# Prompt attention of a two-layer encoder step: the four query tiles of a head in the order 3, 0, 2, 1

## What is computed

```python
def mla_attend(q_nope, q_pe, q_pos, k_nope, k_pe, v, k_pos):
    s = jnp.einsum('bqhd,bkhd->bhqk', q_nope, k_nope) + jnp.einsum('bqhr,bkr->bhqk', q_pe, k_pe)
    s = s.astype(jnp.float32) * MLA_SCALE
    mask = (k_pos[None, :] // CHUNK) <= (q_pos[:, None] // CHUNK)
    s = jnp.where(mask[None, None], s, -jnp.inf)
    p = jax.nn.softmax(s, axis=-1).astype(v.dtype)
    return jnp.einsum('bhqk,bkhv->bqhv', p, v)
```

## Time and profile before

| | us |
|---|---|
| median of three runs | 2980.27 |
| lowest, highest | 2978.68, 2980.59 |
| profiled execution, its own time | 2978.17 |
| profiled execution, span | 2976.2 |

### The profile page before, as it was taken

How to read it: one execution, slowest core, us unless ns; L and a number is a source line. 1 busy time by engine, 2 the same in 40 slices (tenths; PEclk the granted TensorE clock), 3 DMA queues, 4 the chain that set the end, 5 groups by cost and what they waited for, 6 DMA issues and landing times.

```text
span 2976.2 us, 49155 instructions
## 1 busy us (share of the span) xinstructions
PE 2798.5 (94%) x18292; PEld 2660.1 (89%) x18292; DVE 1293.6 (43%) x2187; ACT 939.3 (32%) x1412; POOL 896.1 (30%) x362
## 2 busy tenths in 40 slices
PE   6899999989879989999989999998997998999997
PEld 4799999989867889999989999998986788999996
DVE  7742342462574353232364334245257535323234
ACT  6541221233344332111243222133334533211112
POOL 0233233343110233333343323334321113333333
PEclk8999999989989989999989999998998998999998
DMA  9533333322141112222224233332213201222223
GB/s 337 193 116 100 127 113 104 108 83 81 47 147 44 43 57 78 66 83 71 71 85 143 98 114 127 100 113 85 76 50 116 87 29 57 71 76 80 78 64 106
DMA packets 81891, 284.71 MB, mean 96 GB/s; under 512 B 9963, under 2 KB 12939, under 8 KB 81099
## 3 DMA queue, kind: packets, MB, share of 16 engines
q1 hardware_dynamic: 71307, 259.35, 26.6%
q10 hardware_dynamic: 10432, 23.27, 2.6%
HBM read 276.12 MB, written 6.46 MB: 95 GB/s over the span
## 4 chain that ended last, share of the span: by engine, by line
PE 88%; DVE 5%; issue 4%; ACT 2%; DMA 1%; ACTq 0%; SPq 0%; DVEq 0%
PE bank L887 24%; PE bank L889 24%; PE bank L888 24%; PE bank L896 5%; PE bank L1321 1%; PE bank L1282 1%; PE bank L908 1%; DVE n_lo L1434 1%; PE bank L1294 1%; DVE r_t L1751 1%; PE bank L1311 1%; DVE q_h L1755 1%; PE bank L1038 1%; PE bank L1040 1%; PE bank L1039 1%
## 5 line engine op out<-in xcount | busy, mean ns | idle before, releaser
L442 POOL TENSOR_TENSOR w_lo<-raw,w_hi 128x1024 fp32r<-128x1024 f32 x340 | 856.1, 2530 | 2064.3 <-ACT w_hi L483 2064.3
L887 PE MATMUL bank<-n_hi,w_hi 128*128 128x320 f32 x3264 | 1020.5, 313 | 56.9 <-DVE n_lo L1434 56.9
L888 PE MATMUL bank<-n_lo,w_hi 128*128 128x320 f32 x3264 | 1015.9, 311 | 0.0
L889 PE MATMUL bank<-n_hi,w_lo 128*128 128x320 f32 x3264 | 1015.6, 311 | 0.0
L887 PEld LDWEIGHTS bank<-n_hi,w_hi 128*128 128x128 f32 x3264 | 619.2, 190 | 66.8 <-DVE n_lo L1434 64.0
L888 PEld LDWEIGHTS bank<-n_lo,w_hi 128*128 128x128 f32 x3264 | 619.8, 190 | 1.9
L889 PEld LDWEIGHTS bank<-n_hi,w_lo 128*128 128x128 f32 x3264 | 619.4, 190 | 0.0
L483 ACT CAST w_hi<-raw 128x1024 fp32r<-128x1024 f32 x340 | 346.0, 1046 | 564.4 <-PE bank L889 511.4
L887 PE MATMUL bank<-h_hi,w_hi 128*128 128x320 f32 x1408 | 435.7, 309 | 0.0
L889 PE MATMUL bank<-h_hi,w_lo 128*128 128x320 f32 x1408 | 435.1, 309 | 0.0
L888 PE MATMUL bank<-h_lo,w_hi 128*128 128x320 f32 x1408 | 435.1, 309 | 0.0
(11 more groups left out here) (238 smaller groups left out, 2775.5 us busy)
## 6 DMA issues: line engine op xcount, KB each, us to landing
raw<-in_wmain SPq DMA_DIRECT2D x340, 512.0 KB, 3.6
araw<-in_wada SPq DMA_DIRECT2D x144, 512.0 KB, 4.9
pk_t<-in_pastkT ACTq DMA_DIRECT2D x16, 256.0 KB, 3.9
pv<-in_pastv ACTq DMA_DIRECT2D x16, 256.0 KB, 4.2
x<-in_xT SPq DMA_DIRECT2D x1, 2560.0 KB, 14.9
y<-y_sb SPq DMA_DIRECT2D x1, 2560.0 KB, 7.5
s_s<-in_s ACTq DMA_DIRECT2D x4, 512.0 KB, 4.1
uk_t<-in_ukT ACTq DMA_DIRECT2D x2, 1024.0 KB, 6.2
```

The lines of the kernel that those rows point to most:

```text
L442: pool.tensor_tensor(w_lo[slot][:], raw[slot % 2][:].rearrange("p (c m) -> p c m", m=P), w_hi[slot][:].bitcast(F32), ALU.subtract).then_in ...
L887: pe.matmul(out, w_hi[w][:, c, :], r_hi, start=first, stop=False)
L888: pe.matmul(out, w_hi[w][:, c, :], r_lo, start=False, stop=False)
L889: return pe.matmul(out, w_lo[w][:, c, :], r_hi, start=False, stop=last)
```

## The change

A function gives the query tile of a prompt tile, in the order 3, 0, 2, 1 within each head. The widths of the scores, maximum, exponential, scaling, transposes, copy and values follow it, and so does the place of the queries and of the outputs. The condition under which PE waits for a bank of the previous pair of heads is written by the tile's number, since the first tile of a head is no longer query tile 0. Banks, buffers, semaphores and the rounds of the casts stay as they are.

```diff
+        def q_tile(it):
+
+            return (3, 0, 2, 1)[(it - NDEC) % 4]
...
-                            w = P * ((it - NDEC) % 4 + 1)
+                            w = P * (q_tile(it) + 1)
...
-                            qt = (jt - NDEC) % 4
+                            qt = q_tile(jt)
...
-                        h, qt = (it - NDEC) // 4, (it - NDEC) % 4
+                        h, qt = (it - NDEC) // 4, q_tile(it)
...
-                    src, n = (p_s[it % 4], 3) if it < NDEC else (p_p[it % 4], (it - NDEC) % 4 + 1)
+                    src, n = (p_s[it % 4], 3) if it < NDEC else (p_p[it % 4], q_tile(it) + 1)
...
-                    if h % 2 == 0 and qt == 0:
+                    if (it - NDEC) % 8 == 0:
...
-                            t = p_p[n][:, 0:P * ((jt - NDEC) % 4 + 1)]
+                            t = p_p[n][:, 0:P * (q_tile(jt) + 1)]
```

## The result

| | before | after |
|---|---|---|
| median of 20 runs | 2979.64 | 2983.82 |
| lowest, highest | 2976.9, 2984.7 | 2980.66, 2990.41 |
| profiled execution, its own time | 2978.17 | 2990.41 |
| first prompt scores to output projection, layer 1 | 69.79 | 71.17 |
| the same, layer 2 | 69.79 | 71.16 |

The ratio of the medians is 1.0014, with a 95% interval of 1.0008 to 1.0021, so the change costs between 2.4 and 6.3 us. The forecast was 2983.2 and a move within 0.2%; the move is 0.14%. The profiled execution of after is the slowest of the 20 and 12.2 us above the one of before; only 2.75 us of that lie in the two stretches that the change touches.

A forecast was written before the change was run, and what follows sets the result against it. PE was taken to set the pace, so only its waits count: they rise from 7.36 to 8.82 us a layer, +1.46, or +2.9 over two layers, giving a median of 2983.2 us, range 2979.5 to 2987.

The forecast's parts named there:

- the way in: Start of a layer's prompt part: first scores 512 columns instead of 128, one wait +0.52 us, the next -0.16.
- the samples' o_lo: Second head: the 0.94 us wait behind the samples' subtraction, ahead of q3's transposes before, goes: -0.94 a layer.
- A: Transposes of q1 wait 0.36 us for their scaling, queued on DVE behind the next head's q3 maximum.
- B: Values product of q2 waits 0.36 us for its copy, queued behind q3's maximum and exponential.
- C: Values product of q3 waits 0.14 us for its copy, behind q2's maximum and exponential; 0.56 a layer.
- evictions: After every second head, o_hi cast and o_lo subtraction make q3's transposes wait about 0.54 us; 1.62 a layer.
- the way out: End of a layer's prompt attention, where no scores cover: waits fall from 1.05 to 0.19 us, -0.86.
- PE's blocks: Transposes, values products and scores on PE add up to 6.8 us a head whatever the order.
- the slow one: Rival: eviction lateness carries on to q0's transposes and q3's values, about 1 us more each; 2989.3 us; chance 0.10.
- The hidden eviction: Rival: the eviction stays hidden as before and the way in costs nothing; 2980.1 us; chance 0.12.
- The faster one: Rival: wide beside narrow tiles evens PE's blocks and both q3 waits vanish; 2974.5 us; chance 0.03.
- The clock: Rival: PE's clock falls from 1.00 to half over the prompt attention; 3080 us; chance 0.01.

The follow-up runs named there:

- the kernel without waits: Order 1, 3, 2, 0, scaling ahead of maximum at q2 and q0, copy ahead of exponential at q1, q2, q0: 2967.96 us, the kernel before 2979.97.
- the swaps: Changed kernel, at q3: scaling ahead of maximum, stretch 71.60 us; copy ahead of exponential, 69.14; both, 68.06; changed kernel without them 71.17.
- the two swaps: Old order with the scaling ahead of q3's maximum and the copy ahead of q3's exponential: one run 2973.20 us, stretch 66.69 against 69.79 before.

## Why the prediction was right

The sign, the size and the place hold: the part that the argument covers, +1.46 a layer, is 1.38. That 2983.2 was forecast and 2983.8 measured is in part luck: the forecast started from a median of before of 2980.27 and added 2.9, while the medians of 20 are 2979.64 and 4.2 more, of which the argument covers 2.75.

The terms of the sum, worked out in the same way from the two timelines of layer 1, show how near each came:

| waits of PE in a layer, changed less before | forecast | read from the timelines |
|---|---|---|
| the way in | +0.36 | +0.38 |
| the samples' o_lo | -0.94 | -0.94 |
| six times A and B for the two waits of before | +0.72 | +0.63 |
| C | +0.56 | +0.80 |
| evictions | +1.62 | +1.54 |
| the way out | -0.86 | -0.98 |
| sum | +1.46 | +1.43 |

The stretch itself grew by 1.38; the 0.05 between is rounding over some 60 blocks. So that the sum is off by 0.08 only is luck as well: C was forecast 0.24 too small, and three other terms miss by 0.29 together the other way.

- **PE's blocks** don't depend on the order: 6.8 us a head was forecast, 6.8 is what the kernel without waits shows.
- **A and B** were forecast 0.36 each and are 0.71 together. That they are two chains and not widths is shown by the swaps: A removed alone comes back in B to the hundredth, B removed alone gives 0.35 a head, both give 0.70. Both chains stand behind q3 in the old order too, where the two swaps gave back 0.60 a head; so of the 1.38 between the orders A and B make only the 0.1 a head by which they are longer.
- **C** was mis-sized: 0.14 forecast, 0.22 to 0.23 measured where a pair begins, hence heads of 7.72 for 7.65. The step that failed is the hand-off of 0.05 from the copy's end to V, taken from a V with one wait. A second, long fulfilled wait behind the one for the copy, with the register instruction that it brings, adds 0.08.
- **The eviction**: T(q3) late by 0.54 forecast, 0.51 measured; the head 8.05 against 8.01 to 8.02; moving it gave back 0.37 a pair.
- **The way in**: +0.52 forecast, 0.75 - 0.21 = 0.54 measured; -0.16 forecast and measured. The first head in the old order gives back 0.41, where 0.4 was worked out.
- **The samples' o_lo**: its extra wait is gone, as forecast; no T in the second head of after is later than by wait A.
- **The way out** was mis-sized by 0.12. The last rows of PE, before, then after:

```profile
...
982.17 0.43 PE L1321 MATMUL bank<-pt_p,v_m 128*64 128x128 f32 x2
...
983.87 0.65 PE L1321 MATMUL bank<-pt_p,v_m 128*64 128x128 f32 x4
984.46 0.66 PE L1294 MATMUL bank<-ident,p_p 128*128 128x128 f32 x4
985.04 1.91 PE L1321 MATMUL bank<-pt_p,v_m 128*64 128x128 f32 x14
```

```profile
...
990.80 1.09 PE L1325 MATMUL bank<-pt_p,v_m 128*64 128x128 f32 x8
991.82 0.55 PE L1298 MATMUL bank<-ident,p_p 128*128 128x128 f32 x3
992.30 0.43 PE L1325 MATMUL bank<-pt_p,v_m 128*64 128x128 f32 x2
992.66 0.44 PE L1298 MATMUL bank<-ident,p_p 128*128 128x128 f32 x2
993.03 1.31 PE L1325 MATMUL bank<-pt_p,v_m 128*64 128x128 f32 x10
```

After, T(q2) was forecast 0.13 late and isn't late: it starts 1.02 behind V(q3), which is the length of a V of four blocks with no wait behind it (950.29 to 951.31 in the earlier trace rows). The forecast had counted that V with 0.93. Each of the two V behind a T takes 0.06 more than its T alone accounts for, 0.11 in all for 0.19 forecast. Before, T(q2) at 983.33 waits 0.80 behind 982.17 + 0.36, where 0.95 was taken from the idle shown; but the next two V are 0.12 and 0.06 late, and V(q3), whose first product starts at 985.86 in the trace, is 0.11 late. That makes 1.09 for 1.05 forecast.

The rivals: the slow one needed lateness carried on behind an eviction, but V(q3) behind the eviction of after starts at 959.33, 0.20 behind its T at 959.13, and that T 0.54 behind the scores of 256 columns at 958.59, their own length, so neither waits; that rival is refuted. (The next A, at 962.72, is the ordinary one, so the limit of 0.3 that the forecast set on it couldn't have told this rival.) The hidden eviction is refuted by moving it. The faster one, that evener blocks on PE help by themselves, is refuted for this order: what counts is the cover behind q3. The order 0, 3, 2, 1 is faster, and not because it is even: counted as in the forecast its rounds have 6, 11, 8 and 5 units. Behind q3's scores PE has T 0.31, V 0.80 and S 0.75 there, a cover of 1.86 in place of 1.10 and, in the old order, 0.99. The clock stayed at 1.00:

```profile
...
934.00:994.00 60.00, 55.51 (x322) 35.53 (x323) 29.84 (x92) 29.04 (x93) 0.00 (x0) 1.00 0.00 1
```

That row also shows why the busy share says little: 55.5 of 60 us, where the earlier trace rows has 55.6, though the head is 0.32 to 0.62 longer.

## What to carry to other kernels

In a software pipeline over tiles of unequal size the bound engine waits where an instruction that it needs is queued, on another engine, behind the work of the widest tile, and where its own work in between is narrow. Write down for each such pair the chain (need) and the bound engine's blocks (cover), and choose order and queue places so that every cover exceeds its need; two chains that end at neighbouring instructions are best shortened together: here shortening the first alone gave nothing and the second alone only its own part. Of the three orders run without swaps the best one was not the one with the most even work, but the one with the most work behind its widest tile.

## What the runs showed of the hardware

A wait that has long been fulfilled isn't always free. Where it stood behind the wait that came last, with a register instruction for its value between the two, the values matmul began 0.12 us after the copy's end in the chain of waits instead of 0.04, and moving the fulfilled wait away gave 0.08 back in each of three places. Ahead of the transposes, where the weight load itself carried the wait that came last, the gap was 0.04 with two waits as well.

And the stretch of 70 us repeated within 0.02 us over executions and layers, for two kernels that were profiled twice, while the rest of the kernel spread by 9.4 us over fourteen profiles. A difference such as the 0.24 us of the moved wait can be read in such a stretch from one profile; the medians of the whole kernel, whose intervals here reach 2 to 4 us to either side, can't show it.
